# Sliding-window attention: the pieces of the next projections spread as 10, 6, 11, 2 and 3 over a head, and one weight load behind the totals

## The chip, the cores and the metric

The kernel runs on one core of one Trainium2 chip. The metric is the device time of one execution in microseconds (us), lower is better. The engines are TensorE (PE, with its weight loads as PEld), VectorE (DVE), ScalarE (ACT), GpSimd (POOL) and SyncE (SP), whose queue starts nearly all transfers. Each runs its own list of instructions in order and waits for the others only at semaphores.

## The reference, cut to what matters

The whole program computes two blocks of layers over 1024 tokens with 1024 channels: a gated linear attention, a dilated sliding-window attention (SWA), a differential attention and a latent attention, each with its projections and norms. The change lies in SWA alone, which computes, for each of 8 query heads, three attentions of different stride and blends them by a softmax over their log-sums:

```python
for gi, (window, dilation) in enumerate(((128, 1), (512, 4), (2048, 16))):
    o_g, lse_g = dilated_window_attention(q[:, :, gi], k_sh[:, :, gi], v_sh[:, :, gi], window, dilation)
    ...
wts = jax.nn.softmax(jnp.stack(lses, axis=0), axis=0)
o = jnp.sum(wts[..., None] * jnp.stack(outs, axis=0), axis=0)
return (o.astype(x.dtype) * jax.nn.silu(g)) @ w_out
```

Here `q` and `g` are projections `x @ w_in`, `q` with a rotary turn (rope), `lse_g` is the row maximum plus the logarithm of the sum of exponentials.

## The kernel before, in words

`swa_phase` works head by head. Two key-value heads (`kv` 0 and 1) each serve four query heads: `alone` projects keys, values and the first queries, then `head` runs four times, three times in a hardware loop and once written out. Of the eight heads, seven prepare the projections of what comes next (`nxt` is "q", or "k" in the last head of the first key-value head); the eighth has nothing to prepare.

A head has these stages on TensorE (`fill`, `scores`, `turn_p` and `weighted`, L1294 to L1368):

- **Scores.** Ten steps (`STEPS`: four of stride 1, four of stride 4, two of stride 8) write 512 columns of scores into one of two banks (L1317 to L1320). DVE adds the mask, takes the row maximum and scales it (`shift`, L1523, L1525, L1527); step i of TensorE needs the bank that `shift(i-2)` has read. ACT takes the exponential with its sum (L1424).
- **Log-sums.** After the last step ACT takes the logarithm of the sums (L1453), DVE subtracts the maxima (L1548), TensorE transposes the 96x128 tile (L1356, "the first transposition"), ACT copies it out (L1456), and SP sends the strided groups through HBM into token order (L1187, L1191).
- **Totals.** DVE and ACT blend the three log-sums by token: maximum and differences (L1556 to L1562), exponential (L1461), sums (L1565, L1567), logarithm (L1465), totals (L1571 to L1573). SP sends them through HBM (L1196, L1200), TensorE transposes them back (L1359, "the second transposition"), DVE adds the maxima (L1578), ACT makes the factors (L1469), DVE multiplies the probabilities with them (`normalize`, L1539, ten times).
- **Weighted sums.** For each of ten steps TensorE transposes the probabilities (`turn_p`, L1328), ACT copies them (L1444), TensorE multiplies with the values (`weighted`, L1343, L1347). DVE multiplies the result with the gate (L1586), and the next head begins.

Between these, TensorE does the **pieces** of the next projections: 32 pieces of six matmuls each (L1257 to L1259). Four weight slots make eight pieces each: 0 to 7 the gate of this head, 8 to 15 the queries of stride 1 of the next head, 16 to 23 of stride 4, 24 to 31 of stride 8. The first four pieces of a slot fill one bank of 512 columns, the last four the other; before a bank is filled again it has to be emptied by DVE (`cosine`, called by `turn_q`, L1492) and by ACT (`take`, two half copies L1387 and L1388), or for the gate by L1432 and L1531. Where the pieces go is set by a table and three numbers:

```python
WITH_SCORES = (0, 2, 4, 6, 8, 10, 11, 12, 14, 15, 16)
FIRST_T, COVER, FILL = 20, 28, 30
```

Pieces `WITH_SCORES[i]` to `WITH_SCORES[i+1]` follow score step i, those up to `FIRST_T` come ahead of the first transposition, those up to `COVER` between the two transpositions, those up to `FILL` behind the second, and the rest one by one between the transpositions of the probabilities.

POOL splits a raw weight slot into two parts (`split_slot`, L108 and L110), the split of slot n waiting until TensorE has used slot n-2, and finishes the rope (L1214, L1222). SP loads raw slots (`load`, L1172), each waiting until POOL has split the slot two ahead of it. Within a head POOL's order is: split for pieces 16 to 23; split for 24 to 31; rope of group 0; wait for the totals; split for the next head's gate; wait for the last `normalize`; rope 1; split; rope 2. SP's order is two loads, the log-sums, the totals, two loads.

Of the kernel before, what the change touches and what calls it, by code (L numbers as in the profile page):

```python
# [1093 lines left out]
def swa_phase(nc, g):  # L1094
# [10 lines left out]
    s0 = FIRST["swa"]  # L1105
# [4 lines left out]
    N = len(STEPS)  # L1110
    LAST_OF = [max(i for i in range(N) if STEPS[i][0] == gr) + 1 for gr in range(G)]
    ROPES = G + G * HEADS
    with ExitStack() as ctx:
# [21 lines left out]
        o_half = lambda h, half: g.o_t[:, bass.ds(h, 1), cols[half]].rearrange("p o s -> p (o s)")  # L1135
        by_token = lambda a, r: a.rearrange("t (r i) -> t i r", r=r)
        in_order = lambda a, r: a.rearrange("t (i r) -> t i r", r=r)
        WITH_SCORES = (0, 2, 4, 6, 8, 10, 11, 12, 14, 15, 16)
        FIRST_T, COVER, FILL = 20, 28, 30

        def parts(i):

# [25 lines left out]
        @block.sync  # L1168
        def _(sp):
            def load(slot, u):  # L1170
                sp.wait_ge(g.raw_free, slot + (s0 + 4 - 1))
                sp.dma_start(g.w_raw[:, u, :], g.w_slots[bass.ds(slot + (s0 + 4), 1), :, :].rearrange("o p n -> (o p) n"))\  # L1172
                    .then_inc(g.raw_full[u], 16)

            def alone(kv):
                for kind, j, slot, nz in standalone(kv):
                    load(slot, slot % 2)

            def head(kv, hh, h, nxt):
                z = hh * 4 + (kv * PER_KV + 9)  # L1180
                if nxt:
                    load(z, 1)
                    load(z + 1, 0)

                sp.wait_ge(m.lt_ready, h + 1)
                for n in range(2):
                    sp.dma_start(g.lse_d[n].rearrange("(t p) -> t p", p=P), lse_t[32 * (n + 1):32 * (n + 1) + NT, :]).then_inc(m.lse_out, 16)  # L1187
                sp.wait_ge(m.lse_out, h * 32 + 32)
                for n in range(2):
                    d = SWA_STRIDE[n + 1]  # L1190
                    sp.dma_start(nat[:, n, :].rearrange("t (r i) -> t r i", r=d), g.lse_d[n].rearrange("(r t i) -> t r i", r=d, t=NT))\  # L1191
                        .then_inc(m.lse_in, 16)
                sp.wait_ge(m.total_ready, h + 1)
                for n in range(G):
                    d = SWA_STRIDE[n]
                    sp.dma_start(g.total_d[n].rearrange("(r t i) -> t r i", r=d, t=NT), total[:, n, :].rearrange("t (r i) -> t r i", r=d))\  # L1196
                        .then_inc(m.total_out, 16)
                sp.wait_ge(m.total_out, h * 48 + 48)
                for n in range(G):
                    sp.dma_start(back[32 * n:32 * n + NT, :], g.total_d[n].rearrange("(t p) -> t p", p=P)).then_inc(m.total_in, 16)  # L1200
                if nxt:
                    load(z + 2, 1)
                    load(z + 3, 0)
                else:
                    load(z, 1)

            sequence(sp, alone, head)

        @block.gpsimd
        def _(pool):  # L1210
            def rope(kind, j, nz):

                pool.wait_ge(m.j_act, nz * 2 + 2)
                nc.gpsimd.tensor_tensor(swp[:, j % 2, :], swp[:, j % 2, :], sin[:, :], ALU.mult)  # L1214
                pool.drain()
                if kind == "q":
                    dst, a, b = qs[:, j, :], qs[:, j, :], swp[:, j % 2, :]
                else:
                    d = SWA_STRIDE[j]
                    dst = keys[:, j, :].rearrange("p (r i) -> p r i", r=d)  # L1220
                    a, b = (x.rearrange("p (i r) -> p r i", r=d) for x in (qs[:, j, :], swp[:, j % 2, :]))
                nc.gpsimd.tensor_tensor(dst, a, b, ALU.add).then_inc(m.rope_ready, 1)  # L1222

            def alone(kv):
                for kind, j, slot, nz in standalone(kv):
                    split_slot(nc, pool, g, s0 + slot + 2, 0)
                    if kind != "v":
                        rope(kind, j, nz)

            def head(kv, hh, h, nxt):  # L1230
                z = kv * PER_KV + 9
                nz = hh * G + (kv * (G + ROPES) + 9)
                split_slot(nc, pool, g, s0 + z + 2, hh * 4)
                if nxt:
                    for j in range(G):
                        if j == 1:
                            pool.wait_ge(m.total_ready, h + 1)
                        split_slot(nc, pool, g, s0 + z + 3 + j, hh * 4)
                        if j == 1:
                            pool.wait_ge(m.p_ready, h * N + N)  # L1240
                        rope(nxt, j, nz + j)

            sequence(pool, alone, head)

        @block.tensor
# [127 lines left out]
        def _(act):  # L1373
# [39 lines left out]
            def head(kv, hh, h, nxt):  # L1413
# [31 lines left out]

                for i in range(N):
                    exp(i)
                    if nxt and i in (2, 4):
                        gate(i // 4)
                    if i == 7:  # L1450
                        take(0, 0)
                act.drain()
                nc.scalar.activation(spread(lse[:, :]), dense(den[:, :]), ACT.Ln).then_inc(m.ln_ready, 1)  # L1453
                take(0, 1)
                act.wait_ge(m.lt_done, h + 1)
                nc.scalar.copy(lse_t[:, :], turn(0)[0:96, 0:P]).then_inc(m.lt_ready, 1)  # L1456
                if not nxt:
                    gate(0)
                take(1, 0)
                act.wait_ge(m.terms_ready, h + 1)  # L1460
                nc.scalar.activation(ee[:, :, :], ee[:, :, :], ACT.Exp).then_inc(m.terms_exp, 1)  # L1461
                if not nxt:
                    gate(1)
                act.wait_ge(m.z_ready, h + 1)
                nc.scalar.activation(ee[:, 0, :], ee[:, 0, :], ACT.Ln).then_inc(m.z_ln, 1)  # L1465
                take(1, 1)
                take(2, 0)
                act.wait_ge(m.f_ready, h + 1)
                nc.scalar.activation(dense(fac[:, :]), spread(lse[:, :]), ACT.Exp, scale=-1.0).then_inc(m.fac_ready, 1)  # L1469
                for i in range(N):  # L1470
                    take_p(i)
                    if i == 2:
                        take(2, 1)

            sequence(act, alone, head)

# [1 line left out]
        def _(dve):  # L1478
# [23 lines left out]
            def head(kv, hh, h, nxt):  # L1502
# [37 lines left out]

                for i in range(N):
                    shift(i)
                    if nxt and i in (3, 5):
                        gate(i // 5)
                    if i == 7:
                        turn_q(0, 0)
                dve.wait_ge(m.ln_ready, h + 1)
                nc.vector.tensor_tensor(spread(lse[:, :]), spread(lse[:, :]), dense(nm[:, :]), ALU.subtract).then_inc(m.lse_ready, 1)  # L1548
                if not nxt:
                    gate(0)  # L1550
                turn_q(0, 1)
                turn_q(1, 0)

                d1, d2 = SWA_STRIDE[1], SWA_STRIDE[2]
                dve.wait_ge(m.lse_in, h * 32 + 32)
# [5 lines left out]
                nc.vector.tensor_tensor(in_order(ee[:, 1, :], d1), by_token(nat[:, 0, :], d1), in_order(top[:, :], d1), ALU.subtract)  # L1561
                nc.vector.tensor_tensor(in_order(ee[:, 2, :], d2), by_token(nat[:, 1, :], d2), in_order(top[:, :], d2), ALU.subtract)\  # L1562
                    .then_inc(m.terms_ready, 1)
                dve.wait_ge(m.terms_exp, h + 1)
                nc.vector.tensor_tensor(ee[:, 0, :], ee[:, 0, :], ee[:, 1, :], ALU.add)  # L1565
                dve.drain()
# [6 lines left out]
                nc.vector.tensor_tensor(by_token(total[:, 2, :], d2), in_order(ee[:, 0, :], d2), in_order(top[:, :], d2), ALU.add)\  # L1573
                    .then_inc(m.total_ready, 1)
                turn_q(1, 1)
                turn_q(2, 0)
                dve.wait_ge(m.bt_done, h + 1)
                nc.vector.tensor_tensor(spread(lse[:, :]), spread(turn(1)[:, 0:96]), dense(nm[:, :]), ALU.add).then_inc(m.f_ready, 1)  # L1578
                dve.wait_ge(m.fac_ready, h + 1)
                for i in range(N):  # L1580
                    normalize(i)
                    if i == 4:
                        turn_q(2, 1)
                dve.wait_ge(m.pv_done, h * N + (N + 2))
                o = g.o_t[:, bass.ds(h, 1), :].rearrange("p o s -> p (o s)")
                nc.vector.tensor_tensor(o, o, out, ALU.mult).then_inc(m.o_taken, 1)  # L1586
# [967 lines left out]
```

## Time and profile before

| | us |
|---|---|
| median of 3 runs | 3047.07 (3046.64 to 3048.09) |
| the profiled execution's own time | 3045.38 |
| its span in the profile | 3043.6 |
| PE busy | 2818.4 (93%) |
| DVE busy | 1496.6 (49%) |
| ACT busy | 1185.8 (39%) |
| POOL busy | 952.7 (31%) |
| mean granted TensorE clock | 0.965 |

SWA lies between about 600 and 1335 us of the span; the heads that prepare projections begin at 701.38, 774.13, 848.05, 920.25, 1060.83, 1134.63 and 1206.86 us, the eighth at 1279.04. In the timeline an instruction has its start, its modelled length, its engine and line, and in brackets how long the engine stood idle before it and what released it. Matmuls are pipelined: the time that one costs is the distance from start to start, not its length. An engine's idle time costs something only where it lies on the path that sets the end.

### The profile page before, as it was taken

The numbers are of one execution on the slowest core, as the hardware profiler recorded it, in microseconds if no ns is written. First come the engines' busy times: TensorE is split into PE (matmuls) and PEld (weight loads), VectorE is DVE, ScalarE is ACT, GpSimd is POOL, SyncE is SP. The second block draws the span as 40 slices with busy tenths as digits, with TensorE's granted clock in tenths as the row PEclk, the third lists the DMA queues.
The fourth block names the chain that finished last, engine by engine and source line by source line (L and its number), as shares of the span: only waits on it lengthen the run. The fifth ranks groups of instructions, "written<-read, shape, count | busy, mean of one in ns | idle before, by whom it ended". The sixth has DMA issues, their size and how long they took to land. (4 is left out here: it accounts for less than half of the span.)

```text
span 3043.6 us, 38799 instructions
## 1 busy us (share of the span) xinstructions
PE 2818.4 (93%) x14702; PEld 2310.1 (76%) x14702; DVE 1496.6 (49%) x1968; ACT 1185.8 (39%) x1974; POOL 952.7 (31%) x490
## 2 busy tenths in 40 slices
PE   7999997899999999979799999999699989999988
PEld 5887785688888888766477777777476768888876
DVE  6765565704444144555455655666533325444443
ACT  4123222424444144433445455555523324434432
POOL 3463352154334543331233232333031341000020
PEclk9999998899999999989799999999899999999999
DMA  4224323111000110021111111111041110000021
GB/s 155 89 76 131 117 70 117 70 42 42 28 28 29 42 36 28 28 95 65 58 42 42 28 43 33 37 42 35 8 152 35 42 48 15 8 14 8 9 89 56
DMA packets 57305, 162.33 MB, mean 53 GB/s; under 512 B 8400, under 2 KB 10064, under 8 KB 57168
## 3 DMA queue, kind: packets, MB, share of 16 engines
q1 hardware_dynamic: 49968, 134.17, 13.7%
q10 hardware_dynamic: 7200, 26.22, 2.7%
q8 instruction: 99, 1.62, 0.2%
q14 instruction: 38, 0.31, 0.0%
HBM read 133.99 MB, written 17.99 MB: 50 GB/s over the span
## 5 line engine op out<-in xcount | busy, mean ns | idle before, releaser
L108 POOL TENSOR_SCALAR w_hi<-w_raw 128x1024 fp32r<-128x1024 f32 x126 | 139.2, 1105 | 1499.2 <-PE pj L134 525.0
L110 POOL TENSOR_TENSOR w_lo<-w_raw,w_hi 128x1024 fp32r<-128x1024 f32 x126 | 309.2, 2454 | 19.0 <-issue 5.2
L1257 PE MATMUL pj<-x_hi,w_hi 128*128 128x512 f32 x688 | 285.5, 415 | 4.9 <-ACT swa_swapped L1388 4.9
L1259 PE MATMUL pj<-x_hi,w_lo 128*128 128x512 f32 x688 | 270.9, 394 | 0.0
L1258 PE MATMUL pj<-x_lo,w_hi 128*128 128x512 f32 x688 | 270.3, 393 | 0.0
L132 PE MATMUL pj<-x_hi,w_hi 128*128 128x512 f32 x544 | 220.0, 404 | 11.5 <-DVE gate_cumsum L550 7.5
L1708 PE MATMUL pj<-x_hi,w_hi 128*128 128x512 f32 x496 | 216.8, 437 | 7.1 <-ACT da_raw L1823 7.1
L134 PE MATMUL pj<-x_hi,w_lo 128*128 128x512 f32 x544 | 213.6, 393 | 0.0
L133 PE MATMUL pj<-x_lo,w_hi 128*128 128x512 f32 x544 | 213.4, 392 | 0.0
L1710 PE MATMUL pj<-x_hi,w_lo 128*128 128x512 f32 x496 | 196.2, 396 | 0.0
L1709 PE MATMUL pj<-x_lo,w_hi 128*128 128x512 f32 x496 | 195.3, 394 | 0.0
L1939 DVE TENSOR_REDUCE da_neg_max<-at 128x1 f32<-128x1024 f32 x128 | 150.5, 1217 | 90.3 <-PE at L1736 90.1
L1257 PEld LDWEIGHTS pj<-x_hi,w_hi 128*128 128x128 f32 x688 | 131.0, 190 | 32.4 <-issue 7.8
L1424 ACT ACTIVATE swa_p<-swa_p,swa_neg_max 128x256 f32<-128x256 f32 (+1 forms) x192 | 89.1, 465 | 170.4 <-DVE swa_neg_max L1527 170.4
L782 PE MATMUL pj<-x_hi,out_w_hi 128*128 128x512 f32 x384 | 153.0, 399 | 0.0
L1259 PEld LDWEIGHTS pj<-x_hi,w_lo 128*128 128x128 f32 x688 | 130.1, 189 | 28.7
L783 PE MATMUL pj<-x_lo,out_w_hi 128*128 128x512 f32 x384 | 150.3, 391 | 0.0
L784 PE MATMUL pj<-x_hi,out_w_lo 128*128 128x512 f32 x384 | 150.0, 391 | 0.0
L1258 PEld LDWEIGHTS pj<-x_lo,w_hi 128*128 128x128 f32 x688 | 130.4, 189 | 25.3
L782 PE MATMUL pj<-x_hi,w_hi 128*128 128x512 f32 x176 | 86.6, 492 | 61.4 <-DVE x_lo L929 34.3
L1845 ACT COPY da_p_t<-pj 128x512 f32<-128x512 f32 x128 | 74.9, 585 | 172.8 <-PE pj L1744 168.6
L1754 PEld LDWEIGHTS pj<-da_p_t,da_v 128*128 128x128 f32 x1024 | 129.6, 200 | 14.9 <-ACT da_p_t L1845 10.1
(352 smaller groups left out, 6597.3 us busy)
## 6 DMA issues: line engine op xcount, KB each, us to landing
w_raw<-w_slots SPq DMA_DIRECT2D x158, 512.0 KB, 3.5
o_t<-ada_t ACTq DMA_DIRECT2D x24, 512.0 KB, 3.5
ada_row<-ada_t ACTq DMA_DIRECT2D x24, 512.0 KB, 3.5
x_res<-o_t SPq DMA_DIRECT2D x24, 512.0 KB, 2.7
o_t<-x_res SPq DMA_DIRECT2D x24, 512.0 KB, 6.7
da_swapped<-da_raw SPq DMA_DIRECT2D x64, 128.0 KB, 2.3
o_t<-x_t SPq DMA_DIRECT2D x4, 1024.0 KB, 9.1
o_t<-x_t SPq DMA_DIRECT2D x8, 512.0 KB, 6.8
```

Of the source, the lines that this page charges most:

```text
L110: nc.gpsimd.tensor_tensor(g.w_lo[:, u, :], g.w_raw[:, u, :], g.w_hi[:, u, :], ALU.subtract)\
L132: nc.tensor.matmul(dst, w_hi, x_hi[:, k, cols], start=(j == 0), stop=False)
L133: nc.tensor.matmul(dst, w_hi, x_lo[:, k, cols], start=False, stop=False)
L134: mm = nc.tensor.matmul(dst, w_lo, x_hi[:, k, cols], start=False, stop=(j == n - 1))
L782: nc.tensor.matmul(dst, w_hi[:, w], g.x_hi[:, k, cols[half]], start=(k == 0), stop=False)
L1257: nc.tensor.matmul(proj(half), g.w_hi[:, u, w], g.x_hi[:, k, cols[half]], start=(k == 0), stop=False)
L1258: nc.tensor.matmul(proj(half), g.w_hi[:, u, w], g.x_lo[:, k, cols[half]], start=False, stop=False)
L1259: mm = nc.tensor.matmul(proj(half), g.w_lo[:, u, w], g.x_hi[:, k, cols[half]], start=False, stop=(k == KT - 1))
L1708: nc.tensor.matmul(proj(half), g.w_hi[:, u, w], g.x_hi[:, k, cols[half]], start=(k == 0), stop=False)
L1709: nc.tensor.matmul(proj(half), g.w_hi[:, u, w], g.x_lo[:, k, cols[half]], start=False, stop=False)
L1710: mm = nc.tensor.matmul(proj(half), g.w_lo[:, u, w], g.x_hi[:, k, cols[half]], start=False, stop=(k == KT - 1))
L1939: nc.vector.tensor_reduce(nm[:, col:col + 1], map_banks(c), AX.X, ALU.max, negate=True).then_inc(m.nm_ready, 1)
```

## The change

The pieces are spread anew. With each score step goes one piece (pieces 0 to 9), six follow ahead of the first transposition (10 to 15), eleven stand between the transpositions (16 to 26, before it were eight), two behind the second (27, 28), and three among the transpositions of the probabilities (29 to 31). The steps of ACT and DVE that empty the banks move with the pieces, POOL's wait for the totals moves ahead of the rope of group 0, and SP's second load moves from ahead of the log-sums to behind the totals. No arithmetic is added or removed.

```diff
-        WITH_SCORES = (0, 2, 4, 6, 8, 10, 11, 12, 14, 15, 16)
-        FIRST_T, COVER, FILL = 20, 28, 30
+        WITH_SCORES = range(N + 1)
+        FIRST_T, COVER, FILL = 16, 27, 29
...
                 if nxt:
                     load(z, 1)
-                    load(z + 1, 0)
...
                 if nxt:
+                    load(z + 1, 0)
                     load(z + 2, 1)
                     load(z + 3, 0)
...
                     for j in range(G):
-                        if j == 1:
+                        split_slot(nc, pool, g, s0 + z + 3 + j, hh * 4)
+                        if j == 0:
                             pool.wait_ge(m.total_ready, h + 1)
-                        split_slot(nc, pool, g, s0 + z + 3 + j, hh * 4)
-                        if j == 1:
+                        elif j == 1:
                             pool.wait_ge(m.p_ready, h * N + N)
                         rope(nxt, j, nz + j)
```

On ACT `take(0, 0)` goes behind the logarithm, `take(0, 1)` behind the copy of the log-sums, `take(1, 0)` and `take(1, 1)` behind the logarithm of the blend, `take(2, 0)` and `take(2, 1)` behind `take_p(1)` and `take_p(4)`; the gate's two halves go behind `exp(4)` and `exp(8)`. On DVE `turn_q(0, 0)` and `turn_q(0, 1)` stand behind the subtraction L1548, `turn_q(1, 0)` between the differences and the sums, `turn_q(2, 0)` and `turn_q(2, 1)` behind `normalize(2)` and `normalize(7)`, the gate's halves behind `shift(5)` and `shift(9)`.

DVE in a head of the hardware loop, from the subtraction of the maxima to the first multiplications, before (lines up to L1548 are those of the profile; L1556 to L1573 the blend, L1492 the emptying of a projection bank):

```order
L1548 TENSOR_TENSOR swa_lse<-swa_lse,swa_neg_max 128x3x8
L1491 REGISTER_ALU
L1492 TENSOR_TENSOR swa_q<-pj,swa_cos 128x512
L1489 REGISTER_ALU
L1492 TENSOR_TENSOR swa_q<-pj,swa_cos 128x512
L1555 ISA
L1556 TENSOR_TENSOR swa_top<-swa_lse_t,swa_lse_by_token 8x128
L1558 TENSOR_TENSOR swa_top<-swa_top,swa_lse_by_token 8x128
L1560 TENSOR_TENSOR swa_terms<-swa_lse_t,swa_top 8x128
L1561 TENSOR_TENSOR swa_terms<-swa_lse_by_token,swa_top 8x128
L1562 TENSOR_TENSOR swa_terms<-swa_lse_by_token,swa_top 8x128
L1565 TENSOR_TENSOR swa_terms<-swa_terms 8x128
```

The same place on DVE in the changed kernel, whose lines here are two to four lower (L1490 for L1492, L1552 for L1556, L1562 for L1565), from the first row of the blend:

```order
L1552 TENSOR_TENSOR swa_top<-swa_lse_t,swa_lse_by_token 8x128
L1554 TENSOR_TENSOR swa_top<-swa_top,swa_lse_by_token 8x128
L1556 TENSOR_TENSOR swa_terms<-swa_lse_t,swa_top 8x128
L1557 TENSOR_TENSOR swa_terms<-swa_lse_by_token,swa_top 8x128
L1558 TENSOR_TENSOR swa_terms<-swa_lse_by_token,swa_top 8x128
L1487 REGISTER_ALU
L1490 TENSOR_TENSOR swa_q<-pj,swa_cos 128x512
L1562 TENSOR_TENSOR swa_terms<-swa_terms 8x128
L1564 TENSOR_TENSOR swa_terms<-swa_terms 8x128
L1568 TENSOR_TENSOR swa_totals<-swa_terms,swa_top 8x128
```

The emptying of the first half of the stride 4 queries now stands inside the blend, between the differences and the sums.

SP in a head of the hardware loop, the difference (L1172 a weight load, L1187 and L1191 the log-sums, L1196 and L1200 the totals; in the changed kernel L1186, L1190, L1195 and L1199):

```order
 L1172 DMA w_raw<-w_slots 128x1024
+L1184 REGISTER_ALU
+L1186 DMA swa_group_lse<-swa_lse_t 8x128 x2
+L1187 ISA
+L1190 DMA swa_lse_by_token<-swa_group_lse 8x4x32
+L1190 DMA swa_lse_by_token<-swa_group_lse 8x8x16
+L1195 DMA swa_total_lse<-swa_totals 8x128
+L1195 DMA swa_total_lse<-swa_totals 8x4x32
+L1195 DMA swa_total_lse<-swa_totals 8x8x16
+L1197 ISA
+L1199 DMA swa_total_t<-swa_total_lse 8x128 x3
 L1172 ISA
```

One load stays ahead of the log-sums and three stand behind the totals, where two stood on either side.

POOL in a head of the hardware loop, behind the split for pieces 24 to 31, the difference (L1214 and L1222 are the rope of group 0; L1213 and the register row of L1237 or L1238 belong to the waits):

```order
 L108 TENSOR_SCALAR w_hi<-w_raw 128x1024
 L110 TENSOR_TENSOR w_lo<-w_raw,w_hi 128x1024
-L1213 ISA
-L1214 TENSOR_TENSOR swa_swapped<-swa_swapped,swa_sin 128x1024
-L1222 TENSOR_TENSOR swa_q<-swa_q,swa_swapped 128x1024
-L1237 REGISTER_ALU
+L1238 REGISTER_ALU
+L1213 ISA
+L1214 TENSOR_TENSOR swa_swapped<-swa_swapped,swa_sin 128x1024
+L1222 TENSOR_TENSOR swa_q<-swa_q,swa_swapped 128x1024
```

The rope of group 0 ran ahead of the wait for the totals and now runs behind it, still ahead of the split for the next head's gate.

## Rows read from the trace of the kernel before

**Rows 1.** Waits of PE over the span: waiter, releaser, us in total, times, longest.

```profile
PE pj L1359 <- DMA swa_total_t<-swa_total_lse: 27.1, 8, 9.2
...
PE pj L1257 <- ACT swa_swapped L1388: 4.9, 8, 3.0
```

**Rows 2.** Timeline of PE in the first head: start, length, engine, line.

```profile
740.14 0.27 PE L1356 MATMUL pj<-ident,swa_lse 128*96 128x128 f32 x1
740.66 0.47 PE L1257 MATMUL pj<-x_hi,w_hi 128*128 128x512 f32 x1 [0.25 <-ACT swa_swapped L1388]
...
751.44 0.39 PE L1259 MATMUL pj<-x_hi,w_lo 128*128 128x512 f32 x1
754.84 0.30 PE L1359 MATMUL pj<-ident,swa_total_t 96*128 96x96 f32 x1 [3.00 <-DMA swa_total_t<-swa_total_lse]
...
758.01 0.48 PE L1257 MATMUL pj<-x_hi,w_hi 128*128 128x512 f32 x1
...
759.50 0.60 PE L1328 MATMUL pj<-ident,swa_p 128*128 128x128 f32 x4
```

**Rows 3.** Timeline of PE in the eighth head.

```profile
1301.98 0.29 PE L1356 MATMUL pj<-ident,swa_lse 128*96 128x128 f32 x1
1302.06 0.47 PE L1257 MATMUL pj<-x_hi,w_hi 128*128 128x512 f32 x1
```

**Rows 4.** Timeline of SP's queue, first and eighth head: start, length of the issues.

```profile
750.73 0.96 SPq L1196 DMA_DIRECT2D swa_total_lse<-swa_totals  x3
752.72 0.94 SPq L1200 DMA_DIRECT2D swa_total_t<-swa_total_lse  x3
...
1302.60 0.64 SPq L1187 DMA_DIRECT2D swa_group_lse<-swa_lse_t  x2
1304.17 0.62 SPq L1191 DMA_DIRECT2D swa_lse_by_token<-swa_group_lse  x2
```

**Rows 5.** Timeline of DVE in the first, third and eighth head.

```profile
725.75 0.69 DVE L1523 TENSOR_TENSOR swa_p<-at,swa_band 128x512 f32<-128x512 f32 x1 [0.54 <-PE at L1320]
...
745.91 0.38 DVE L1556 TENSOR_TENSOR swa_top<-swa_lse_t,swa_lse_by_token 8x128 f32<-8x128 f32 x1 [4.88 <-DMA swa_lse_by_token<-swa_group_lse]
...
748.62 0.28 DVE L1567 TENSOR_TENSOR swa_terms<-swa_terms 8x128 f32<-8x128 f32 x1
...
755.65 3.10 DVE L1539 TENSOR_TENSOR swa_p<-swa_p,swa_factors 128x512 f32<-128x512 f32 x5 [0.29 <-ACT swa_factors L1469]
...
891.27 1.21 DVE L1556 TENSOR_TENSOR swa_top<-swa_lse_t,swa_lse_by_token 8x128 f32<-8x128 f32 x1 [3.54 <-DMA swa_lse_by_token<-swa_group_lse]
...
1305.91 0.39 DVE L1556 TENSOR_TENSOR swa_top<-swa_lse_t,swa_lse_by_token 8x128 f32<-8x128 f32 x1 [0.71 <-DMA swa_lse_by_token<-swa_group_lse]
...
1309.22 2.43 DVE L1567 TENSOR_TENSOR swa_terms<-swa_terms 8x128 f32<-8x128 f32 x1
```

**Rows 6.** Timeline of POOL, end of the first head and the eighth head.

```profile
765.40 2.36 POOL L1214 TENSOR_TENSOR swa_swapped<-swa_swapped,swa_sin 128x1024 f32<-128x1024 f32 x1 [10.89 <-DVE swa_p L1539]
...
771.42 2.35 POOL L110 TENSOR_TENSOR w_lo<-w_raw,w_hi 128x1024 fp32r<-128x1024 f32 x1
...
1309.16 2.34 POOL L110 TENSOR_TENSOR w_lo<-w_raw,w_hi 128x1024 fp32r<-128x1024 f32 x1
```

**Rows 7.** Timeline of ACT in the first head: the logarithm of the blend.

```profile
749.55 0.31 ACT L1465 ACTIVATE swa_terms<-swa_terms 8x128 f32<-8x128 f32 x1
```

**Rows 8.** Timeline of PE: second transposition and next head, second and third head.

```profile
827.17 0.30 PE L1359 MATMUL pj<-ident,swa_total_t 96*128 96x96 f32 x1 [2.55 <-DMA swa_total_t<-swa_total_lse]
...
848.05 0.44 PE L1317 MATMUL at<-swa_k,swa_q 128*128 128x128 f32 x2
...
900.96 0.30 PE L1359 MATMUL pj<-ident,swa_total_t 96*128 96x96 f32 x1 [2.44 <-DMA swa_total_t<-swa_total_lse]
...
920.25 0.44 PE L1317 MATMUL at<-swa_k,swa_q 128*128 128x128 f32 x2
```

**Rows 9.** Window in the second head: busy time (count) of PE, PEld, DVE, ACT, POOL, granted clock.

```profile
830.00:832.00 2.00, 2.00 (x9) 1.51 (x7) 1.23 (x3) 0.00 (x0) 0.00 (x0) 0.54 0.02 6
```

More of the change, by code:

```diff
@@ L1447, in head @@
                     exp(i)
[L1448 to L1451, printed above, removed]
+                    if nxt and i in (4, 8):
+                        gate(i // 8)
                 act.drain()
                 nc.scalar.activation(spread(lse[:, :]), dense(den[:, :]), ACT.Ln).then_inc(m.ln_ready, 1)
-                take(0, 1)
+                take(0, 0)
                 act.wait_ge(m.lt_done, h + 1)
@@ L1458, in head @@
                     gate(0)
-                take(1, 0)
+                take(0, 1)
                 act.wait_ge(m.terms_ready, h + 1)
@@ L1465, in head @@
                 nc.scalar.activation(ee[:, 0, :], ee[:, 0, :], ACT.Ln).then_inc(m.z_ln, 1)
+                take(1, 0)
                 take(1, 1)
-                take(2, 0)
                 act.wait_ge(m.f_ready, h + 1)
@@ L1471, in head @@
                     take_p(i)
-                    if i == 2:
-                        take(2, 1)
+                    if i in (1, 4):
+                        take(2, i // 4)
             sequence(act, alone, head)
@@ L1542, in head @@
                     shift(i)
[L1543 to L1546, printed above, removed]
+                    if nxt and i in (5, 9):
+                        gate(i // 9)
                 dve.wait_ge(m.ln_ready, h + 1)
@@ L1550, in head @@
                     gate(0)
+                turn_q(0, 0)
                 turn_q(0, 1)
-                turn_q(1, 0)
                 d1, d2 = SWA_STRIDE[1], SWA_STRIDE[2]
@@ L1563, in head @@
                     .then_inc(m.terms_ready, 1)
+                turn_q(1, 0)
                 dve.wait_ge(m.terms_exp, h + 1)
@@ L1575, in head @@
                 turn_q(1, 1)
-                turn_q(2, 0)
                 dve.wait_ge(m.bt_done, h + 1)
@@ L1581, in head @@
                     normalize(i)
-                    if i == 4:
-                        turn_q(2, 1)
+                    if i in (2, 7):
+                        turn_q(2, i // 7)
                 dve.wait_ge(m.pv_done, h * N + (N + 2))
```

## The prediction

> **What bounds the kernel now.** I read the page first: TensorE is busy 93% of the span and no other engine over half, so only time in which TensorE stands can be won. Then its waits [rows 1]: of the two that lie in the heads, the second transposition L1359 waits for the totals' transfer, 27.1 us in eight heads, 9.2 of them in the eighth, which the change leaves alone; 17.9 us are left in seven. The first piece behind the first transposition waits for ACT's bank copy L1388, 4.9 us less one wait of 3.0 outside the heads. Third, PE's timeline of the first head [rows 2], which shows where: T is the start of the first transposition (740.14), T2 that of the second (754.84), and between them stand eight pieces. Last, the other engines from T to T2 [rows 4, 5, 6, 7]: a chain through ACT, two round trips over HBM, and the blend on DVE and ACT. It takes 14.7 us, the pieces cover about 11.5.
>
> **The change, part by part.**
>
> *What the waits cost.* The eight pieces are 48 matmuls; from 740.66 to 751.44 there are 47 distances, 0.229 us each [rows 2], so a piece costs 1.37. From the last matmul to L1359 are 3.40 us where 0.23 would be normal: 3.17 lost, where the idle time says 3.00. With 0.17 more for each of seven, 17.9 becomes 19.1. Behind the first transposition the next matmul starts after 0.52 us [rows 2]; in the eighth head, where no bank is awaited, after 0.08 [rows 3]. That is 0.44 times seven, 3.1. Together 22.2 us can be won.
>
> *More cover.* Eleven pieces instead of eight: 11.01 (740.66 to one distance past 751.44) and 3 x 1.37, with the 0.08 ahead, put TensorE at the second transposition at T+15.2.
>
> *The chain.* Before, it took 14.70. The eighth head shows it without a weight load ahead of the log-sums and without POOL's rope: from T (1301.98) to the second transfer's issue (1304.17) 2.19, and to L1556 (1305.91) 1.74 more [rows 3, 4, 5], so T+3.93. From there the first head's steps, where L1556 was not held (0.38): 745.91 to the totals' issue 750.73 is 4.82, to T2 4.11 [rows 2, 4, 5]. Sum T+12.9. In the third head L1556 took 1.21 with the rope beside it; the rope now comes after the totals. Nearest-row bounds are 12.9 and 14.7; I take 13, because both things that lengthened it are moved. Either is less than 15.2, so the wait at L1359 goes in both cases.
>
> *DVE's inserted bank step.* `turn_q(1, 0)` now stands between differences and sums. It needs piece 19, done at T+0.08+4 x 1.37 = T+5.6, when the differences are about done. An instruction of this shape takes 0.69 [rows 5], so the sums come at most 0.7 later. The logarithm L1465 started 0.65 after the sums ended (748.62 and 0.28, against 749.55), because ACT was loading its table [rows 5, 7]: the table load hides nearly all of it. Cost 0; without that cover 0.7, inside the margin of 2.3.
>
> *ACT's bank copies.* `take(1, 0)` is queued behind that logarithm, whose end is 0.87 ahead of the totals' issue (749.86 and 750.73) [rows 4, 7]: T+3.93+4.82-0.87 = T+7.9. Piece 24 needs the bank at T+0.08+8 x 1.37 = T+11.0. Three us are left for two half copies: cost 0. Piece 16 now waits for a bank that ACT and DVE empty while pieces 12 to 15 run, so the 0.44 goes too. `take(1, 1)` has until piece 28, behind T2.
>
> *SP.* The load moves past two log-sum writes, two reads, three total writes and three reads. It now goes out 2.93 us behind the totals' first issue (752.72 and 0.94, less 750.73) [rows 4], T+11.7, and POOL wants that slot only behind the last multiplication, which ends after T2+0.8+6.2 = T+22. The two loads queued behind it wait for POOL's later splits anyway. Had it stayed, SP would stand until the split of pieces 24 to 31, which now begins only at T, with the log-sums behind it. Cost 0.
>
> *POOL and the multiplications.* Behind the totals (T+8.75) POOL now does a rope and a split, 8.4 us as from 765.40 to 773.77 [rows 6], ending at about T+17.3 with its start. The first multiplication L1539 would start 0.81 behind T2, T+16.0 [rows 2, 5]. In the eighth head L1567, with both inputs in SBUF, took 2.43 instead of 0.28 and ended with POOL's L110, 1311.65 and 1311.50 [rows 5, 6]. If L1539 is held likewise, it ends at T+17.3 and 0.62 (a fifth of 3.10), T+17.9; `turn_p(0)` wants it at T2+0.1+2 x 1.37 = T+18.0. Bounds: 0, and 0.8 per head if the totals are a us later. I take 0.15, nearer the computed times: 1.0 us. The trace shows such a hold on 8x128 tiles only. The Trainium skill, "SBUF — State Buffer", section "Who interferes with whom", says that a DVE instruction with two SBUF inputs contends with a GpSimd instruction that reads SBUF, whatever the shape; it speaks against putting POOL's split there. By it the 1.0 stands or grows; if the large tiles were not held, the sum would be 1.0 better.
>
> *Pieces that stand alone.* A single piece among transpositions costs 1.49 (758.01 to 759.50) [rows 2] against 1.37, and there is one more of them: 0.12 x 7 = 0.8. In the score steps pieces only leave; DVE, which sets the pace behind them, still stood 0.54 in a step with one piece [rows 5]. Cost 0.
>
> *The clock.* In the second head TensorE stood 2.55 us; from 830 to 832 the granted clock was 0.54, near its 1.2 GHz level, and from T2 to the next head passed 20.88 us against 19.29 in the third head [rows 8, 9]: 1.6 lost. By the starts in the table above, the fifth head too is 1.6 longer than the third (73.80 and 72.20). Both falls came behind this wait, so I take them back: 3.2. Bounds: 0 and 3.2. The Trainium skill, "TensorE: Matmul & The Clock Gate", section "What's actually happening", has the throttled state as the default that activity lifts; by it no fall follows once the wait is gone, and the 3.2 come; if the falls had another cause, the sum would be 3.2 worse.
>
> *Sum.* -22.2 +0.8 +1.0 -3.2 = -23.6. Against the profiled execution's 3045.4 that gives 3021.8; it lies 1.7 below the median of the runs, so **3023.5 us**.
>
> **The rivals.**
>
> 1. *Part is lost behind T2.* POOL holds the subtraction's successor and the multiplications 0.8 us per head (4.6 more), piece 24 waits 0.3 (2.1), and the clock falls stay (3.2): 3033.4. For it: the multiplication's margin is 0.1 us. Against: one late start lets DVE in between POOL's two parts.
> 2. *The round trip stays as long as before*, 14.7 and 0.7 for the inserted step: T+15.4, a wait of 0.2; the logarithm then ends at T+10.4, two half copies later (nearly 1.2) piece 24 is 0.6 late. 0.8 x 7 = 5.6 less: 3029.1. For it: the load's part in the length is read off one head.
> 3. *DVE sets the pace of the shortened score steps.* Its spare 0.54 is small, and POOL can hold its L1527. One POOL part of 2.34 [rows 6] as a wait per head takes 16.4 back: 3039.9, next to no change. Against: TensorE runs a bank ahead.
> 4. *Slower: the blend is held, with the bank copy behind it.* If POOL's split for pieces 24 to 31, which now begins only at T, slides by 2 us, it lies on the blend: L1556 0.83 and L1567 2.15 longer [rows 5]. With the old chain's logarithm at T+9.7 and the 0.7, ACT empties the bank at about T+14.6, and piece 24 waits 3.6 us. It decides from a wait of 3.0. Price: 7 x 3.6 = 25.2 for the 22.2 won, 0.8, and clock falls in all seven heads instead of two, 8.0: 11.8 slower, 3058.9. For it: the split ends close to L1556 even undisturbed. Against: nothing delays it, its weights were loaded a head ago.
>
> **Chances.** The forecast 67%, rival 1 15%, rival 2 10%, rivals 3 and 4 4% each. A measurement here can tell 0.2%, 6.1 us, from no change. The forecast and rivals 1 and 2 lie beyond it, rival 3 about at the border: 0.91 faster, 0.05 same, 0.04 slower. The range goes from 3020 (no hold, 1.0; no waits; the spread of the runs) to 3033.5, rival 1.
>
> **What would show it.** Right: no wait at L1359 in the seven heads and 9.2 in the eighth; no wait behind L1356; from T to T2 15.2; the totals' issue at T+8.75; L1556 at 0.38; from head to head about 69.4 (72.2 less 2.9 plus 0.1); granted clock 1.00 throughout the heads. Wrong: a wait of TensorE at piece 24 (rivals 2 and 4), at the first transpositions of probabilities (rival 1), or at the score steps for L1523 (rival 3).

## The result and the profile after

The changed kernel takes **3019.28 us** (median of 4 runs, 3014.53 to 3023.58) against 3047.49 (4 runs, 3046.64 to 3048.09) for the kernel before: ratio 0.9907, 95% interval 0.9887 to 0.9927. It is faster, as forecast, by 28.2 us where 23.6 were forecast, and 0.7 us below the lower end of the forecast range. Two of the four runs lie at 3014.53 and 3015.28, two at 3023.27 and 3023.58, and the median falls between them. The profiled execution is one of the shorter two, 3015.28, with a span of 3013.5. In two later sets of runs the changed kernel took 23.5 us less than the kernel before (3023.05 against 3046.54) and 28.4 less (3019.31 against 3047.68).

Waits of TensorE in the changed kernel, in the form of [rows 1]:

```profile
PE pj L1359 <- DMA swa_total_t<-swa_total_lse: 9.3, 1, 9.3
...
PE pj L1257 <- ACT swa_swapped L1388: 3.0, 1, 3.0
```

Both waits left are the ones that the change doesn't touch, L1359 in the eighth head and the one of 3.0 outside the heads. Timeline of TensorE in the changed kernel, first head, as [rows 2], with the starts of heads 2, 3 and 4:

```profile
734.82 0.27 PE L1356 MATMUL pj<-ident,swa_lse 128*96 128x128 f32 x1
734.85 0.48 PE L1257 MATMUL pj<-x_hi,w_hi 128*128 128x512 f32 x1
...
749.95 0.25 PE L1359 MATMUL pj<-ident,swa_total_t 96*128 96x96 f32 x1
749.97 0.48 PE L1257 MATMUL pj<-x_hi,w_hi 128*128 128x512 f32 x1
...
754.80 0.66 PE L1328 MATMUL pj<-ident,swa_p 128*128 128x128 f32 x4
...
770.99 0.44 PE L1317 MATMUL at<-swa_k,swa_q 128*128 128x128 f32 x2
...
840.23 0.44 PE L1317 MATMUL at<-swa_k,swa_q 128*128 128x128 f32 x2
...
909.39 0.44 PE L1317 MATMUL at<-swa_k,swa_q 128*128 128x128 f32 x2
```

From T to T2 it is 15.13 us without a gap, and a head takes 69.2. The next matmul stands 0.03 and 0.02 behind the transpositions, nearer than the 0.08 and 0.10 assumed from the trace of before.

SP's queue, first and second head (start, length of the issues), as [rows 4]:

```profile
735.41 0.67 SPq L1186 DMA_DIRECT2D swa_group_lse<-swa_lse_t  x2
737.02 0.62 SPq L1190 DMA_DIRECT2D swa_lse_by_token<-swa_group_lse  x2
745.28 0.95 SPq L1195 DMA_DIRECT2D swa_total_lse<-swa_totals  x3
...
804.89 0.64 SPq L1186 DMA_DIRECT2D swa_group_lse<-swa_lse_t  x2
806.46 0.62 SPq L1190 DMA_DIRECT2D swa_lse_by_token<-swa_group_lse  x2
813.10 0.95 SPq L1195 DMA_DIRECT2D swa_total_lse<-swa_totals  x3
```

The second head's totals go out at T+8.81 (T is 804.29 there), against T+8.75 worked out. The first head's go out at T+10.46, because the read of the log-sums, from its issue (L1190) to the blend's first step (L1552), took 3.43 us there and 1.82 in the second head. The DVE timeline shows that step (first head, then the second head's multiplications):

```profile
740.45 0.38 DVE L1552 TENSOR_TENSOR swa_top<-swa_lse_t,swa_lse_by_token 8x128 f32<-8x128 f32 x1 [4.75 <-DMA swa_lse_by_token<-swa_group_lse]
...
742.16 0.67 DVE L1490 TENSOR_TENSOR swa_q<-pj,swa_cos 128x512 f32<-128x512 f32 x1
742.82 0.28 DVE L1562 TENSOR_TENSOR swa_terms<-swa_terms 8x128 f32<-8x128 f32 x1
...
750.70 4.65 DVE L1537 TENSOR_TENSOR swa_p<-swa_p,swa_factors 128x512 f32<-128x512 f32 x3 [0.29 <-ACT swa_factors L1467]
...
820.15 3.33 DVE L1537 TENSOR_TENSOR swa_p<-swa_p,swa_factors 128x512 f32<-128x512 f32 x3 [0.29 <-ACT swa_factors L1467]
```

POOL's timeline in the first head:

```profile
745.45 2.40 POOL L1214 TENSOR_TENSOR swa_swapped<-swa_swapped,swa_sin 128x1024 f32<-128x1024 f32 x1 [6.68 <-DVE swa_totals L1570]
748.00 2.39 POOL L1222 TENSOR_TENSOR swa_q<-swa_q,swa_swapped 128x1024 f32<-128x1024 f32 x1
750.36 1.05 POOL L108 TENSOR_SCALAR w_hi<-w_raw 128x1024 fp32r<-128x1024 f32 x1
751.55 2.65 POOL L110 TENSOR_TENSOR w_lo<-w_raw,w_hi 128x1024 fp32r<-128x1024 f32 x1
```

The blend runs free (0.38), the inserted bank step costs nothing (L1562 follows at once), and the first multiplications are held beside POOL: three take 4.65 and 3.33 us, where three take 1.90 with POOL idle, as in the fourth and fifth experiments.

ACT in the first head, the blend's logarithm and the bank copy behind it, and TensorE's first matmul of piece 24, which needs that bank:

```profile
744.10 0.31 ACT L1463 ACTIVATE swa_terms<-swa_terms 8x128 f32<-8x128 f32 x1
...
745.02 0.58 ACT L1388 COPY swa_swapped<-pj 64x512 f32<-64x512 f32 x1
...
745.84 0.39 PE L1257 MATMUL pj<-x_hi,w_hi 128*128 128x512 f32 x1
```

The bank is free at 745.60 (T+10.78) and piece 24 starts at T+11.02: 0.2 us were to spare. In the other six heads the copy ends at T+9.0 to 9.2 and 1.9 are to spare.

**Where the 30.1 us between the two spans lie.** From the start of the first head to that of the eighth it was 577.66 us and is 552.93: 24.7. Up to the first head nothing has changed (0.2 later), from the eighth head to the last projection of the differential attention (DA) 1.2 us are gone, and behind the latent attention's first matmul 1.2 are added. The rest, 5.6, lies between two places that the change doesn't touch: the last DA projection (now L1704, before L1708) and the first matmul of the latent attention (L2187, L2191), 395.0 us before and 389.4 now. Instances of these lines (shortest, mean, longest in ns; start of the first to start of the last), in the kernel before and then in the changed kernel:

```profile
L1708 PE MATMUL pj<-x_hi,w_hi x496: 389/398/777, 1497.6 to 2129.8; 128*128 128x512 f32 x166
...
L2191 PE MATMUL at<-x_hi x128: 389/393/783, 2524.8 to 2918.7; 128*128 128x512 f32 x128
```

```profile
L1704 PE MATMUL pj<-x_hi,w_hi x496: 389/398/795, 1473.8 to 2104.1; 128*128 128x512 f32 x166
...
L2187 PE MATMUL at<-x_hi x128: 389/393/628, 2493.5 to 2887.2; 128*128 128x512 f32 x128
```

### The profile page after: what moved, and what is told of

Its sections match the earlier page's. It is cut to its first block and busy times, and to the rows that moved or that the text cites. A ratio compares the mean times of both kernels' runs of the same rounds, so it can differ in the third digit from the quotient of the medians.

```text
span 3013.5 us, 38793 instructions
## 1 busy us (share of the span) xinstructions
PE 2809.1 (93%) x14702; PEld 2303.8 (76%) x14702; DVE 1501.9 (50%) x1968; ACT 1185.2 (39%) x1974; POOL 951.4 (32%) x490
## 5 line engine op out<-in xcount | busy, mean ns | idle before, releaser
L1704 PE MATMUL pj<-x_hi,w_hi 128*128 128x512 f32 x496 | 216.2, 436 | 7.1 <-ACT da_raw L1819 7.1
L782 PE MATMUL pj<-x_hi,out_w_hi 128*128 128x512 f32 x384 | 153.1, 399 | 0.0
L1259 PEld LDWEIGHTS pj<-x_hi,w_lo 128*128 128x128 f32 x688 | 129.6, 188 | 28.4
L1258 PEld LDWEIGHTS pj<-x_lo,w_hi 128*128 128x128 f32 x688 | 129.9, 189 | 24.7
L782 PE MATMUL pj<-x_hi,w_hi 128*128 128x512 f32 x176 | 87.2, 495 | 61.1 <-DVE x_lo L929 33.6
L1490 DVE TENSOR_TENSOR swa_q<-pj,swa_cos 128x512 f32<-128x512 f32 x60 | 41.3, 689 | 202.0 <-PE pj L1259 201.5
L862 ACT ACTIVATE out_squares<-o_t 128x512 f32<-128x512 f32 x64 | 40.5, 633 | 253.1 <-DVE o_t L950 119.9
```

Of the source, the lines that this page charges most:

```text
L782: nc.tensor.matmul(dst, w_hi[:, w], g.x_hi[:, k, cols[half]], start=(k == 0), stop=False)
L1258: nc.tensor.matmul(proj(half), g.w_hi[:, u, w], g.x_lo[:, k, cols[half]], start=False, stop=False)
L1259: mm = nc.tensor.matmul(proj(half), g.w_lo[:, u, w], g.x_hi[:, k, cols[half]], start=False, stop=(k == KT - 1))
L1704: nc.tensor.matmul(proj(half), g.w_hi[:, u, w], g.x_hi[:, k, cols[half]], start=(k == 0), stop=False)
```

## The experiments

**The changed kernel again**, beside the next three (no edit).

> The changed kernel unchanged. The changed kernel's first profile is 30.1 us shorter in span than that of before; the seven heads and what lies between them account for 24.7, and 5.6 lie between the last differential-attention projection and the latent attention, whose waits are the same. Its four runs lie at 3015 and at 3023 us. Theory A (the 5.6 us are clock falls that land by chance in later stages): the runs again lie in two groups about 8 us apart, and a profile of the slower group has the same 69.2 us per head and a longer later stage with a lower granted clock. Theory B (the change shortens the later stage too): every run is near 3015 and the later stage is 5.6 us shorter in each profile.

Measured: 3023.05 us (6 runs, 3021.15 to 3027.00), 0.9924 [0.9909, 0.9938] of before, which spread from 3041.94 to 3054.03 in 19 runs of that set. In the heads it repeats the first execution: 552.59 from first to eighth start, against 552.93. The 5.6 us behind the DA projections are not there:

```profile
L1704 PE MATMUL pj<-x_hi,w_hi x496: 387/398/797, 1474.8 to 2107.1; 128*128 128x512 f32 x166
...
L2187 PE MATMUL at<-x_hi x128: 389/393/747, 2502.1 to 2896.0; 128*128 128x512 f32 x128
```

That is 395.0, the same as before, with the same kernel. What differs is the granted clock. The stretch from the last DA projection to the first L782, which both executions reach after a wait of 6.47 us, holds 287 matmuls in each. It takes 70.0 us in the first execution and 74.6 in this one (busy time and count of PE, PEld, DVE, ACT, POOL; granted clock, DMA share, GB/s):

```profile
2104.10:2174.10 70.00, 45.79 (x287) 33.44 (x285) 38.96 (x52) 41.22 (x67) 5.07 (x4) 0.87 0.03 8
```

```profile
2107.10:2181.70 74.60, 50.35 (x287) 37.44 (x285) 39.00 (x52) 41.28 (x67) 5.08 (x4) 0.81 0.03 8
```

So 4.6 of the 5.6 us are lost there, at a granted clock of 0.81 instead of 0.87: of eight groups of sixteen matmuls (L1750) two took 3.39 and 3.79 us instead of 2.05 in the first execution, and four took 3.32 to 3.78 in this one, with the same waits ahead of them (0.7 to 1.1 us). The recorded Theory A was right about the clock in a later stage and wrong about the runs: these six make no two groups 8 us apart. In all nine profiled executions of this document the stretch takes between 389.4 and 395.0 us, 390.4 in the second experiment and 393.5 in the third.

**The load back ahead of the log-sums.**

```diff
                     load(z, 1)
+                    load(z + 1, 0)
...
                 if nxt:
-                    load(z + 1, 0)
                     load(z + 2, 1)
```

> The changed kernel with the second weight load put back ahead of the log-sums. Theory (SP's order is binding, because POOL's split of pieces 24 to 31 now begins only at the first transposition T): the log-sums leave 4.3 us later (T+4.7 to 5.0 instead of T+0.62), the blend's logarithm ends at about T+12.3, ACT empties the bank at T+13.5, TensorE waits 2.5 us at piece 24 in each of seven heads, and the time is 17 to 20 us above the changed kernel. Rival (the load matters only by sharing the transfer engines): the log-sums' round trip is 0.4 us longer, hidden by the cover, no change.

Measured: 3058.68 us (3056.39 to 3061.54, 6 runs), 1.0041 [1.0026, 1.0055] of before and 35.6 over the changed kernel, where 17 to 20 were expected. Waits of TensorE:

```profile
PE pj L1257 <- ACT swa_swapped L1388: 25.9, 7, 4.0
...
PE pj L1257 <- DVE swa_q L1490: 3.9, 1, 3.9
```

The first of them in TensorE's timeline (T at 735.37):

```profile
750.35 0.51 PE L1257 MATMUL pj<-x_hi,w_hi 128*128 128x512 f32 x1 [3.81 <-ACT swa_swapped L1388]
```

SP's queue in the first and the second head:

```profile
739.57 0.34 SPq L1172 DMA_DIRECT2D w_raw<-w_slots  x1
740.02 0.67 SPq L1187 DMA_DIRECT2D swa_group_lse<-swa_lse_t  x2
743.38 0.62 SPq L1191 DMA_DIRECT2D swa_lse_by_token<-swa_group_lse  x2
...
814.53 0.33 SPq L1172 DMA_DIRECT2D w_raw<-w_slots  x1
814.97 0.64 SPq L1187 DMA_DIRECT2D swa_group_lse<-swa_lse_t  x2
818.52 0.62 SPq L1191 DMA_DIRECT2D swa_lse_by_token<-swa_group_lse  x2
```

The load waits for POOL's split and goes out first at T+4.20, the log-sums at T+4.65. Directly behind the load the write takes 3.36 and 3.55 us from its issue to the next one (3.07 to 3.66 in the seven heads), where it takes 1.61 and 1.57 in the changed kernel. So piece 24 waits 3.8 to 4.0 us in six heads and 3.45 in the seventh, where the write took 3.07. Each wait is followed by a fall of the clock; windows of the first head:

```profile
748.00:750.00 2.00, 0.00 (x0) 0.00 (x0) 1.01 (x5) 1.95 (x4) 0.00 (x0) 1.00 0.00 0
750.00:752.00 2.00, 1.65 (x5) 1.33 (x6) 0.44 (x1) 1.79 (x4) 1.88 (x1) 0.68 0.05 6
752.00:754.00 2.00, 2.00 (x6) 1.61 (x5) 0.00 (x0) 0.95 (x1) 1.86 (x2) 0.50 0.03 6
```

A head takes 75.0 instead of 69.2: 3.8 for the wait, and 2.0 behind it, near the 1.6 that a fall to the 1.2 GHz level cost in the kernel before [rows 8, 9]. From first to eighth start it is 593.04, 40.5 more than the 552.59 of the changed kernel beside it; the stretch behind the DA projections took 4.6 less here (390.4 against 395.0). The load's place decides the sign of the whole change. The expectation missed by two terms: the wait was 2.5 in it, because the write that lengthens behind the load was left out, and the falls of the clock, 2.0 in each of seven heads, were not in it at all.

**The load alone moved**, in the kernel before.

```diff
                     load(z, 1)
-                    load(z + 1, 0)
...
                 if nxt:
+                    load(z + 1, 0)
                     load(z + 2, 1)
```

> The kernel before with only the load moved behind the totals, pieces as before. Theory (the load's transfer lengthens the log-sums' writes): the write takes 1.57 instead of 1.76 to 2.06 us, the wait at L1359 falls from 17.9 to about 15.4 us in seven heads, the time by 2.5 us or 0.08%. Rival (the load costs the round trip nothing): no change. Second rival (the load is half of the gain): 10 us or more.

Measured: 3044.57 us (3038.54 to 3048.94, 12 runs), 0.9993 [0.9983, 1.0002]; the wait at L1359 stays (27.2 in eight heads). POOL's timeline in the second head, the rope's second half:

```profile
814.58 2.39 POOL L1222 TENSOR_TENSOR swa_q<-swa_q,swa_swapped 128x1024 f32<-128x1024 f32 x1
```

And DVE's, the blend's first step:

```profile
815.71 1.50 DVE L1556 TENSOR_TENSOR swa_top<-swa_lse_t,swa_lse_by_token 8x128 f32<-8x128 f32 x1 [3.25 <-DMA swa_lse_by_token<-swa_group_lse]
```

The write is 0.36 shorter (1.57 instead of 1.93), the step starts that much earlier and stands 0.37 longer, until the rope ends. From the write's issue to the totals' issue it is 9.38 us in both kernels (813.62 to 823.00 before, 812.27 to 821.65 here). The load's share in the round trip is hidden behind POOL's rope. The first head is the exception: its wait fell from 3.00 to 2.54. Alone, the move is worth nothing that shows. The runs by themselves couldn't tell the expected 2.5 us from none (the interval reaches from 5.2 less to 0.6 more), but the waits in the seven heads sum to 17.8 against 17.9 before, where 15.4 was expected.

**The rope of group 0 ahead of the totals**, in the changed kernel.

```diff
-                        if j == 0:
+                        if j == 1:
                             pool.wait_ge(m.total_ready, h + 1)
-                        elif j == 1:
+                        split_slot(nc, pool, g, s0 + z + 3 + j, hh * 4)
+                        if j == 1:
                             pool.wait_ge(m.p_ready, h * N + N)
```

> The changed kernel with POOL's rope of group 0 back ahead of the wait for the totals, so that it runs from about T+4.1 to T+9.0, beside the blend. Theory (POOL holds DVE instructions with two SBUF inputs): L1552 to L1564 take up to 4.9 us longer, the logarithm ends near T+12.5, TensorE waits up to 3 us at piece 24 per head, and the time is 10 to 21 us above the changed kernel. Rival (the cover of eleven pieces has 2.3 us to spare and hides it): no wait at all, and 1.7 us less because the multiplications are no longer held.

Measured: 3039.16 us (3032.30 to 3043.80, 8 runs), 16.1 over the changed kernel of the same set, within the 10 to 21 expected, 0.9970 [0.9955, 0.9984] of before. DVE in the first head:

```profile
743.34 1.36 DVE L1552 TENSOR_TENSOR swa_top<-swa_lse_t,swa_lse_by_token 8x128 f32<-8x128 f32 x1 [4.63 <-DMA swa_lse_by_token<-swa_group_lse]
744.77 2.45 DVE L1554 TENSOR_TENSOR swa_top<-swa_top,swa_lse_by_token 8x128 f32<-8x128 f32 x1
```

POOL in the first head:

```profile
742.07 2.39 POOL L1214 TENSOR_TENSOR swa_swapped<-swa_swapped,swa_sin 128x1024 f32<-128x1024 f32 x1 [0.29 <-issue]
744.60 2.39 POOL L1222 TENSOR_TENSOR swa_q<-swa_q,swa_swapped 128x1024 f32<-128x1024 f32 x1
```

Both halves of the rope hold the blend, each DVE step ending 0.2 us behind a POOL one; in the six other heads it is L1554 and L1556 that are held (2.42 to 2.53 and 2.37 to 2.38 us). The totals go out at T+13.4 (T at 737.82, issue at 751.19), the bank behind them comes late, and piece 24 waits 2.2 to 2.6 us in each of the seven heads; a head takes 71.6. The rival, that eleven pieces cover it, falls; its second half holds, for three multiplications take 1.90 here in the first six heads.

**The split behind the products**, so that nothing of POOL lies beside the multiplications.

```diff
                     for j in range(G):
+                        if j == 1:
+                            pool.wait_ge(m.p_ready, h * N + N)
                         split_slot(nc, pool, g, s0 + z + 3 + j, hh * 4)
...
-                        elif j == 1:
-                            pool.wait_ge(m.p_ready, h * N + N)
```

> The changed kernel with POOL's split of the next head's gate behind the wait for the last multiplication, so that nothing of POOL's runs beside the multiplications. Theory (the hold of the multiplications costs TensorE 0.24 us at the second transposition of probabilities in the first head, and little in the others): in the first head turn_p(0) to turn_p(1) shrinks from 1.97 to about 1.75 us and the time falls by 0.2 to 1.5 us, not to be told from none. Rival (POOL's work then runs 3.5 us further into the next head and holds the row-maximum step L1525 there until TensorE waits for a score bank): 0.5 to 3 us more per head, 3 to 20 us in all.

Measured: 3020.74 us (3018.65 to 3021.81, 5 runs), 0.9910 [0.9896, 0.9923] of before. The third copy of the changed kernel, in the same set, had 3019.31: the two can't be told apart. The first head's multiplications, and then POOL, DVE and TensorE in the eighth head:

```profile
752.89 1.90 DVE L1537 TENSOR_TENSOR swa_p<-swa_p,swa_factors 128x512 f32<-128x512 f32 x3 [0.29 <-ACT swa_factors L1467]
...
1258.83 2.34 POOL L1214 TENSOR_TENSOR swa_swapped<-swa_swapped,swa_sin 128x1024 f32<-128x1024 f32 x1 [0.27 <-issue]
1259.03 2.17 DVE L1525 TENSOR_SCALAR swa_neg_max<-swa_neg_max 128x2 f32<-128x2 f32 x1
...
1261.84 2.07 PE L1320 MATMUL at<-swa_k,swa_q 128*128 128x256 f32 x4 [2.48 <-DVE swa_p L1521]
```

With nothing of POOL's beside them three multiplications take 1.90 in all seven heads, and in the first head the second `turn_p` stands 1.72 behind the first (expected 1.75). From T2 to the next head it is 20.73 us in each of the six heads that another one follows directly, and the seven heads take 552.03 from first to eighth start. Against the changed kernel's three executions, counted from T2 to the next start, that is 0.9, 0.6 and 1.1 us less: the price of the hold. The rival's mechanism comes as well, but costs something only in the eighth head, whose first score steps have no pieces between them: POOL's rope, now later, holds L1525 there for 2.17 us, TensorE waits 2.48, and the head's first transposition comes 24.45 us behind its start instead of 22.14. That gives back more than the split won.

**A cover of nine pieces**: eight pieces ahead of the first transposition, nine behind it.

```diff
-        FIRST_T, COVER, FILL = 16, 27, 29
+        FIRST_T, COVER, FILL = 18, 27, 29
```

> The changed kernel with FIRST_T at 18: ten pieces with the scores, eight ahead of the first transposition T, nine between the two, so that a cover of 12.3 us stands against a chain of 12.9. Theory (ACT empties the stride 4 bank only behind the blend's logarithm, at about T+9.2, so the bank binds ahead of the totals): TensorE waits 0.8 us at piece 24, due at T+8.3, and not at L1359; a head is 70.0 us instead of 69.2, 5 to 6 us in all. Rival (the totals' transfer binds): no wait at piece 24, 0.5 us at L1359, 3 to 4 us in all. Second rival (the chain is shorter than the cover of nine too): no wait and no difference.

Measured: 3028.27 us (3021.53 to 3036.89, 6 runs), 0.9941 [0.9924, 0.9958] of before. L1359 waits in no head but the eighth; piece 24 waits in all seven, 2.37 us in the first head and 0.6 to 0.9 in the others, and a head takes 70.4 (the first 72.1). That is 9.0 over the changed kernel of the same set, 9.3 from first to eighth start, where 5 to 6 were expected: the waits are 6.5 of it, and the multiplications, 1.8 us nearer to POOL's rope, are held longer (4.5 to 4.7 us for three, about 1 in all). Theory and rival differ in where TensorE waits, and it waits where the theory said: the bank behind the blend's logarithm binds before the totals do, so two pieces of the eleven are there for the bank.

**The changed kernel a third time.**

> The changed kernel unchanged, a third profile, beside the others of this call. Theory A (later stages differ by where the clock falls): the seven heads again take 69.1 to 69.4 us each, and from the last differential-attention projection (L1704) to the first latent-attention score (L2187) the span is either about 389.5 or about 395 us, whichever the median of the runs turns out to be; the runs lie between 3013 and 3028. Theory B (the first profile's 389.4 us belongs to the changed kernel): 389.4 again.

Measured: 3019.31 us (3017.41 to 3023.65, 5 runs), 0.9911 [0.9897, 0.9925]; 553.41 from first to eighth start, and 392.3 in the stretch behind the DA projections. That is neither of the two values that Theory A named, so the stretch has more than two lengths, and Theory B falls too. The first head takes 69.68, those behind it 69.2 to 69.3. There T2 is at T+15.31, 0.2 later than in every other head: the log-sums' read took 3.71 us, the bank copy ended at 746.30 (745.72 and 0.58), and piece 24 started behind it, at 746.36. So the first head stands at the edge: 0.2 us to spare at the bank in one execution, 0.2 lost in another.

## Why the prediction was right, and where it was not

*The waits (22.2) and the cover.* Right: T2 at T+15.13 (worked out 15.2), no wait in the seven heads.

*The chain.* Right from the second head on: the totals go out at T+8.71 to 8.84 against 8.75 worked out. In the first head it is 1.7 longer, which the 2.3 us of room at the second transposition took. That both lengtheners had to go is shown: of the 23.5 us that the change is worth in that set, 16.1 are gone with the rope back, and all of them and 12.1 more with the load back (3058.68 against 3046.54 of before).

*The inserted step, the bank copies and SP.* Cost 0, as forecast. ACT's table load (742.80, 1.28 us in the first head) does cover the inserted step: the logarithm follows it at 744.10, while the sums ended at 743.45. But the room is smaller than the 2.3 us that the text works with. The bank for piece 24 is the tighter place: copied at T+10.78 in the first head, needed at T+11.02.

*The multiplications.* The hold is there and strikes 128x512 tiles too, which the trace of before did not show; the Trainium skill, "SBUF — State Buffer", section "Who interferes with whom", which has a DVE instruction with two SBUF inputs contend with a GpSimd instruction that reads SBUF, had it right. By the fifth experiment it costs the heads 0.6 to 1.1 us in all, forecast 1.0.

*The clock in the heads.* Right: granted clock 1.00 and no head more than 0.4 us longer than the next, where before the second and fifth were 1.6 longer each. That the wait made the clock fall was argued from two heads; that no fall follows without it holds in the seven heads of all three executions of the changed kernel.

*The sum in the heads.* Forecast 23.6, measured 24.7 in the first execution (25.1 and 24.3 in the other two, from 577.66 less 552.59 and 553.41). The term left out is the spacing at the transpositions: the next matmul stands 0.03 and 0.02 behind them instead of 0.08 and 0.10, about 0.13 a head, 0.9 in all.

*The step that failed* is the place of everything outside the heads in the working. The sum has no term for it, which puts it at 0, and the lower end of the range, "no hold, 1.0; no waits; the spread of the runs", leaves 2.5 us for it (3023.5 less 1.0 less 3020); the three runs of before had shown a spread of 1.45. As falls of the clock it counted only those in the heads. The runs showed more. Whole gain less the gain in the heads of the profiled execution is 28.2 less 24.7, 3.5 us, in the first set; 23.5 less 25.1, 1.6 the other way, in the second; 28.4 less 24.3, 4.1, in the third. (The gain in the heads rests on the one profile of before.) Runs of before spread over 12 us in the set of 19, and the changed kernel's medians were 3019.28, 3023.05 and 3019.31 in three sets, 15 runs from 3014.53 to 3027.00. Of the 30.1 us between the two profiled spans 5.6 lie in a stretch that no part of the change touches and that the same kernel ran in 389.4, 395.0 and 392.3 us. So the mechanism was right and the size in the heads was off by 1.1; most of the 4.2 by which the median fell below the forecast of 3023.5 lies outside the heads. In the second set the gain met the forecast to 0.1, with the heads 1.5 better and the rest 1.6 worse, which is luck. What makes TensorE's clock fall and return at other places of that stretch stays open: the executions differ in nothing that was set.

*The rivals.* Rival 1's hold is real but at a tenth to a fifth of its price of 5.6. Rivals 2 and 3 didn't come; a part of 3, POOL holding the scaling of the row maximum until TensorE waits, came in the eighth head of the fifth experiment. Rival 4 was the right mechanism at the wrong place: it put the delay at POOL's split; with the load ahead of the log-sums, SP's queue brings the same late blend, a wait of 3.8 for its 3.6, clock falls in all seven heads, and 3058.68 for its 3058.9. That the totals agree so well is luck, for the heads were 15.4 longer than before (593.04 against 577.66) where the rival adds 11.8. The change avoids it by the order on SP.

## What to carry to other kernels

Moving work into a wait only pays if the chain that ends the wait doesn't lengthen with it: list every queue that the chain crosses (here SP's issues, POOL beside DVE, ACT's bank copies) and move what stands ahead of it in the same edit, since each such move alone may show no gain and still be what the edit rests on. Look for the tightest of the places that wait for the chain; here it was a bank and not the transfer at the chain's end. Before giving a narrow range, look for places behind the edit where the clock is already low; their length varies from run to run by more than the terms being argued about. A range needs the spread of many runs, not of three.

## What the runs showed of the chip that was not expected

- The log-sums' write to HBM, two of 4 KB, takes 1.57 us to the next issue on the same queue with nothing ahead, 1.93 with a 512 KB load issued 1.92 us ahead (second head of before: load at 811.70, write at 813.62), and 3.07 to 3.66 with the load issued 0.39 to 0.45 ahead (seven heads of the second experiment). One write with nothing ahead took 2.95, in the first head of the third experiment.
- The log-sums' round trip, from the write's issue to the blend's first step, is 5.04, 4.79 and 5.32 us in the first head of the three executions of the changed kernel, and 3.39, 3.29 and 3.38 in the second; 5.08 and 3.81 in the kernel before; but 5.16 and 5.26 with the load directly ahead. In the changed kernel it is the read that is longer in the first head (3.43, 3.18 and 3.71 us, against 1.71 to 1.90 in the six heads behind it). Why is open.
- A wait of TensorE of 3.4 to 4.0 us was followed by a fall of the clock in seven heads of seven (second experiment), one of 2.4 to 3.0 in two of seven (the kernel before, and two others of seven in the third experiment), one of 2.2 to 2.6 (the rope ahead of the totals) in none. The length of the wait alone doesn't decide: 3.00 us in the first head of before passed without a fall, and 2.41 us in the third head of the third experiment did not.
- DVE slips in between two POOL instructions that follow one another: in the first head of the fourth experiment L1552 ended at 744.70, 0.24 us behind POOL's first half, and L1554, which started at 744.77 beside the second half, ended at 747.22, 0.23 behind that one.
